# Evictions and rotations of the first attention block a step behind their pieces, the latent roots in four stages, another order of pieces

## The chip, the cores and the metric

The kernel runs on one core of a Trainium2 chip. The metric is the device time of one execution in microseconds, as the median of several runs. A core has TensorE (PE; matmuls, with a granted clock of 1.2 or 2.4 GHz), VectorE (DVE), ScalarE (ACT), GpSimd (POOL) and SyncE (SP, which issues the loads here). Each engine works through its own list of instructions in order; semaphores tie the lists together.

## The reference

Three transformer layers on 512 tokens of width 1024. The change lies in the mixer of the first:

```python
h = x @ w_in
c_q, c_kv, k_rope, q_s, k_s, v_s = _split(h, EVEN_SPLIT)      # 384, 256, 32, 512, 128, 128
q = (_rms_norm(c_q, q_norm) @ w_uq).reshape(B, S, 8, 64 + 32)
q_rope = _apply_rope(q[..., 64:], cos, sin)
kv = (_rms_norm(c_kv, kv_norm) @ w_ukv).reshape(B, S, 8, 64 + 64)
k_rope = _apply_rope(k_rope[:, :, None, :], cos, sin)[:, :, 0]
o_mla = _mla_attend(q_nope, q_rope, k_nope, k_rope, v)         # causal
o_swa = _swa_attend(q_s, k_s, v_s, sinks, rel_bias)            # window 128, 8 heads, 2 kv heads
m = jnp.concatenate([o_mla, o_swa], axis=-1) @ w_out
```

What follows (layer norms, MLPs, a second layer with forgetting attention, a third with four branches) is the same before and after.

## The kernel before

**Layout.** Activations stand transposed, features on the partitions and the 512 tokens in the free dimension. A weight tile is up to 8 blocks of 128 x 128. Each operand is split in a high and a low fp32r part: ScalarE writes the high part of a tile (WH, L357), VectorE the low part (WL, L363), and TensorE multiplies three times per block (L393 to L395: high by high, high by low of x, low by high). These three matmuls are a *piece*. A tile passes through one of four slots (RAW, WH, WL); `hi_ahead` and `lo_ahead` work three tiles ahead of the stream's tile `st.n`. Semaphores per slot are `loaded`, `hi_done`, `lo_done` and `used` (TensorE is through with the tile).

**Banks.** Linear outputs alternate between the PSUM banks 0 and 1 (`st.m % 2`). The first matmul of an output waits on `evac[b]` until the output before the last has been evicted. Evictions: VectorE for k, kr, uq and os; ScalarE for v, q, cq, ckv and ukv, the last in two copies, to K96 and VT. PB[2..3] hold scores, PB[4..5] transposed probabilities, PB[6] the values' result. PB[7] serves everything small, one user after the other in the order of `misc_keys` (`pe_misc` waits on `misc_free` of the one before): vector transposes, band turns, sums of squares ("var"), the products that swap halves for the rotation ("kswap", "qswap"), and turns of V ("v4").

**The attention loop.** 32 steps: sliding window (SWA) for 4 pairs of heads by 4 query blocks, then latent attention (MLA) the same. In step c, TensorE (`pe_attend`) does the scores of step c + 1, with query block 0 the values of the pair before, the transposes of step c (L494, which wait for the normalised probabilities, `probs_n`), and then `between(c)`: QUOTA[c] pieces from a list of work, FIRST before the loop, WITH_SWA in steps 0 to 15, WITH_MLA in 16 to 31. ScalarE copies transposed probabilities (L606) and makes exponentials (L582, L586), then runs `between(c)`. VectorE normalises step c (L597), takes the minimum or maximum of step c + 1 (L562, L568), subtracts the low half of an output at query block 0 (L626), then runs `between(c)`.

**Events.** ENDED[c] lists the pieces of work that end in step c. In `between(c)`, ScalarE and VectorE go through ENDED[c] in order; for each they first split the tile three ahead, then wait for TensorE to finish the piece, and evict it:

```python
            def mixer_between(c):
                for ev in ENDED[c]:
                    event(*ev)
```

"var" on VectorE is the reciprocal root (`rsqrt_dve`, L690 to L697) and the scalings of the latent (L2228); "split" the high and low parts of the scaled latent. `vectors` on VectorE copies the transposed vectors and prepares SINK, which the first SWA minimum reads.

SyncE loads the tiles in the order of TILES_A, which follows the lists, each when the low part of the tile four before is done; between the first four tiles and the rest it issues the band and 23 small loads.

## Time and profile before

| | us |
|---|---|
| median of 3 runs | 2456.65 (2456.44 to 2456.81) |
| profiled execution | 2457.71 |
| its span, first to last instruction | 2455.9 |
| TensorE busy | 2274.6 (93%) |
| mean granted clock of TensorE | 0.957 |
| first matmul of step 0's pieces | 56.33 |
| first output matmul from MLA's result (OMH) | 268.98 |

The profile is of one execution; times in it count from the first instruction. In the timeline each row is a start, a duration, the engine and line, and in brackets the idle time before it with what ended it. Matmuls overlap, so the distance of starts tells their rate.

### The profile page before, as it was taken

The page shows a single profiled execution, that of the slowest core. Times are in us where ns is not written, and L with a number is a line of the kernel's source. Part 1 is how long each engine was busy: PE and PEld are TensorE (multiplying, and loading weights), DVE is VectorE, ACT ScalarE, POOL GpSimd, SP SyncE. Part 2 cuts the span into 40 slices and gives each one's busy share as a digit, 9 for nine tenths or more (in the row PEclk, how much of TensorE's full clock was granted, in tenths as well). Part 3 has the DMA queues.
Part 4 walks back from the last instruction along what each step waited for, and adds up shares of the span by engine and source line. Part 5 has one row for each costly group of instructions (what it writes and reads, how often), then busy time and mean ns, then how long its engine had stood idle before and what let it go on. Part 6 is the DMA issues. An engine that isn't in the chain of part 4 may idle for free.

```text
span 2455.9 us, 28046 instructions
## 1 busy us (share of the span) xinstructions
PE 2274.6 (93%) x10190; PEld 1767.6 (72%) x10192; DVE 1263.6 (51%) x1966; ACT 895.2 (36%) x1479; POOL 368.3 (15%) x228
## 2 busy tenths in 40 slices
PE   7879799999999999899999888999969897999998
PEld 5646588888776676688888676467658675888886
DVE  4466553243464444642443664268569558443344
ACT  3444443143244453431332453322343233332333
POOL 0000420001320002400003500133022164000001
PEclk9999999999999999999999989879989898999999
DMA  5012133333233232233332332123211131333322
GB/s 163 17 36 65 52 86 103 102 94 96 67 93 107 69 86 69 69 102 103 92 97 81 91 90 71 35 62 98 74 39 56 43 99 52 104 88 107 95 70 77
DMA packets 360224, 196.43 MB, mean 80 GB/s; under 512 B 12575, under 2 KB 355372, under 8 KB 360124
## 3 DMA queue, kind: packets, MB, share of 16 engines
q1 hardware_dynamic: 360124, 195.10, 27.8%
q8 instruction: 62, 1.02, 0.2%
q14 instruction: 38, 0.31, 0.0%
HBM read 192.93 MB, written 2.14 MB: 79 GB/s over the span
## 4 chain that ended last, share of the span: by engine, by line
PE 81%; DVE 10%; ACT 4%; issue 2%; POOL 1%; SPq 1%; DMA 1%; DVEq 0%; ACTq 0%; POOLq 0%
PE PB L393 20%; PE PB L395 20%; PE PB L394 20%; PE PB L1284 3%; PE PB L1286 2%; PE PB L1285 2%; PE PB L494 2%; PE PB L475 2%; PE PB L521 1%; PE PB L1312 1%; PE PB L1361 1%; DVE WL L363 1%; ACT WH L357 1%; PE PB L1269 1%; ACT PR L582 1%
## 5 line engine op out<-in xcount | busy, mean ns | idle before, releaser
L393 PE MATMUL PB<-XH,WH 128*128 128x512 f32 (+1 forms) x1344 | 539.2, 401 | 45.1 <-DVE XL L785 23.2
L394 PE MATMUL PB<-XL,WH 128*128 128x512 f32 (+1 forms) x1344 | 532.0, 396 | 0.0
L395 PE MATMUL PB<-XH,WL 128*128 128x512 f32 (+1 forms) x1344 | 531.4, 395 | 0.0
L357 ACT ACTIVATE WH<-RAW 128x1024 fp32r<-128x1024 f32 (+2 forms) x379 | 380.3, 1007 | 411.3 <-PE PB L395 370.3
L373 DVE TENSOR_TENSOR WL<-RAW,WH 128x1024 fp32r<-128x1024 f32 x192 | 252.5, 1315 | 186.8 <-ACT WH L357 177.0
L393 PEld LDWEIGHTS PB<-XH,WH 128*128 128x128 f32 (+1 forms) x1344 | 257.3, 191 | 106.8 <-issue 48.7
L395 PEld LDWEIGHTS PB<-XH,WL 128*128 128x128 f32 (+1 forms) x1344 | 256.6, 191 | 56.7 <-issue 1.0
L394 PEld LDWEIGHTS PB<-XL,WH 128*128 128x128 f32 (+1 forms) x1344 | 257.3, 191 | 53.3 <-issue 0.8
L363 DVE TENSOR_TENSOR WL<-RAW,WH 128x1024 fp32r<-128x1024 f32 (+3 forms) x135 | 168.7, 1252 | 160.7 <-ACT WH L357 160.4
L395 PE MATMUL PB<-HH,WL 128*128 128x512 f32 x512 | 199.2, 389 | 0.0
L393 PE MATMUL PB<-HH,WH 128*128 128x512 f32 x512 | 199.2, 389 | 0.0
L394 PE MATMUL PB<-HL,WH 128*128 128x512 f32 x512 | 199.2, 389 | 0.0
L363 POOL TENSOR_TENSOR WL<-RAW,WH 128x1024 fp32r<-128x1024 f32 (+1 forms) x48 | 101.1, 2115 | 417.2 <-ACT WH L357 417.0
L751 POOL TENSOR_TENSOR SM<-ACC 128x512 f32<-128x512 f32 x4 | 5.2, 1292 | 917.7 <-DVE ACC L2287 532.5
L606 ACT ACTIVATE PT<-PB 128x256 f32<-128x256 f32 (+3 forms) x160 | 65.5, 411 | 166.0 <-PE PB L494 165.9
L1796 ACT ACTIVATE HS<-HR 128x512 f32<-128x512 f32 x64 | 40.5, 632 | 197.1 <-DVE HR L2305 197.1
L1284 PE MATMUL PB<-XH,WH 128*128 128x512 f32 x256 | 107.2, 419 | 4.6 <-ACT RS L1902 3.4
L394 PEld LDWEIGHTS PB<-HL,WH 128*128 128x128 f32 x512 | 96.1, 188 | 20.1
L395 PEld LDWEIGHTS PB<-HH,WL 128*128 128x128 f32 x512 | 96.1, 188 | 19.9
L393 PEld LDWEIGHTS PB<-HH,WH 128*128 128x128 f32 x512 | 96.1, 188 | 19.8
L494 PE MATMUL PB<-ID,PR 128*128 128x128 f32 x368 | 65.1, 295 | 41.8 <-DVE PR L597 41.1
L1285 PE MATMUL PB<-XL,WH 128*128 128x512 f32 x256 | 103.1, 403 | 0.0
(485 smaller groups left out, 3582.7 us busy)
## 6 DMA issues: line engine op xcount, KB each, us to landing
RAW<-in_w_up SPq DMA_DIRECT2D x64, 512.0 KB, 4.1
RAW<-in_w_down SPq DMA_DIRECT2D x64, 512.0 KB, 3.8
RAW<-in_w_ffn_gate_up SPq DMA_DIRECT2D x44, 512.0 KB, 3.8
RAW<-in_w_gate SPq DMA_DIRECT2D x32, 512.0 KB, 4.0
RAW<-in_od_w_in SPq DMA_DIRECT2D x24, 512.0 KB, 6.3
RAW<-in_w_in SPq DMA_DIRECT2D x24, 512.0 KB, 4.0
RAW<-in_ple_w_gate SPq DMA_DIRECT2D x16, 512.0 KB, 4.0
RAW<-in_w_ffn_down SPq DMA_DIRECT2D x16, 512.0 KB, 3.9
```

What stands on the lines that cost most here:

```text
L357: act.activation(WH[:, s, 0:nb], RAW[:, s, 0:nb], ACT.Copy).then_inc(hi_done[s], 1)
L363: eng.tensor_tensor(WL[:, s, 0:nb], RAW[:, s, 0:nb], WH[:, s, 0:nb].bitcast(F32), ALU.subtract).then_inc(lo_done[s], 1)
L373: dve.tensor_tensor(WL[:, s], RAW[:, s], WH[:, s].bitcast(F32), ALU.subtract).then_inc(lo_done[s], 1)
L393: pe.matmul(PB[b][0:m, 0:n], WH[:, s, k, 0:m], rh[:, kk, :], start=kk == 0, stop=False)
L394: pe.matmul(PB[b][0:m, 0:n], WH[:, s, k, 0:m], rl[:, kk, :], start=False, stop=False)
L395: x = pe.matmul(PB[b][0:m, 0:n], WL[:, s, k, 0:m], rh[:, kk, :], start=False, stop=kk == last)
L475: xs[e] = pe.matmul(PB[2 + e][:, lo:lo + w], q[:, qb * P:qb * P + P], k[:, ks[0] * P:ks[0] * P + w], start=True, stop=plain)
L494: x = pe.transpose(PB[4 + e][:, c * P:c * P + P], PR[:, e, c * P:c * P + P], ID[:])
L606: done(act.activation(PT[:, e, ks[0]:ks[0] + len(ks), qb * P:qb * P + P], PB[4 + e][:, 0:len(ks) * P].rearrange("p (j q) -> p j q", q=P), ...
L1284: pe.matmul(PB[m % 2][:], WH[:, n % 4, k], XH[:, k], start=k == 0, stop=False)
L1285: pe.matmul(PB[m % 2][:], WH[:, n % 4, k], XL[:, k], start=False, stop=False)
L1286: x = pe.matmul(PB[m % 2][:], WL[:, n % 4, k], XH[:, k], start=False, stop=k == DT - 1)
```

## The change

- The lists have another order: cq 0 is computed before the loop, ahead of the two vector transposes, which now come after the band turns; uq 2, 4 and 5 come earlier, turns and rotations are spread otherwise, and QUOTA is new (4, 4 and 2 pieces in steps 10 to 12, for example).
- In `between(c)`, ScalarE and VectorE first run the events of ENDED[c - 1], then split the tiles three ahead of those in ENDED[c] (`high_next`, `low_next`). An eviction, rotation or turn thus comes one step after its piece. Tile and bank are looked up by name (N_A, M_A).
- "var" and "split" become four stages: "var" (ScalarE's Ln and Exp), then one step later each "norm" (VectorE's root and scalings), "high" and "low". In ENDED they stand ahead of the pieces that end in the same step.

```diff
--- before.py
+++ after.py
@@ -785,29 +785,34 @@
...
-        FIRST = [("k", 0), ("v", 0), ("q", 0), ("q", 1)]
-        WITH_SWA = [("cq", 0), ("cq", 1), ("cq", 2), ("q", 2), ("ckv", 0), ("var", "cq"), ("ckv", 1), ("split", "cq"), ("q", 3),
-                    ("var", "ckv"), ("kr", 0), ("split", "ckv"), ("uq", 0), ("uq", 1), ("kswap", 0), ("qswap", 0), ("ukv", 0),
-                    ("qswap", 1), ("ukv", 1), ("uq", 2), ("uq", 3), ("qswap", 2), ("qswap", 3)]
-        WITH_MLA = [("v4", 0), ("ukv", 2), ("ukv", 3), ("os", 0), ("v4", 1), ("os", 1)]
-        WITH_MLA += [("uq", 4), ("uq", 5), ("qswap", 4), ("ukv", 4), ("qswap", 5), ("ukv", 5), ("os", 2), ("v4", 2), ("os", 3)]
-        WITH_MLA += [("uq", 6), ("uq", 7), ("qswap", 6), ("ukv", 6), ("qswap", 7), ("ukv", 7), ("os", 4), ("v4", 3)]
-        WITH_MLA += [("os", 5), ("os", 6), ("os", 7)]
-        PIECES = {"cq": 8, "ckv": 8, "q": 8, "kr": 8, "uq": 3, "ukv": 2, "os": 4, "split": 0}
-        QUOTA = [6, 6, 6, 6, 6, 6, 5, 6, 6, 5, 6, 6, 5, 4, 4, 4, 5, 5, 5, 5, 5, 4, 4, 4, 4, 4, 4, 3, 3, 3, 3, 3]
-        ENDED = [[] for _ in QUOTA]
-        c = total = 0
+        FIRST = [("k", 0), ("v", 0), ("q", 0), ("q", 1), ("cq", 0)]
+        WITH_SWA = [("cq", 1), ("cq", 2), ("q", 2), ("var", "cq"), ("ckv", 0), ("ckv", 1), ("q", 3), ("var", "ckv"), ("kr", 0),
+                    ("uq", 0), ("uq", 1), ("uq", 2), ("kswap", 0), ("qswap", 0), ("ukv", 0), ("qswap", 1), ("ukv", 1),
+                    ("uq", 3), ("qswap", 2), ("uq", 4), ("qswap", 3), ("uq", 5)]
+        WITH_MLA = [("v4", 0), ("ukv", 2), ("ukv", 3), ("qswap", 4), ("os", 0), ("os", 1), ("v4", 1), ("ukv", 4), ("qswap", 5), ("ukv", 5)]
+        WITH_MLA += [("uq", 6), ("uq", 7), ("v4", 2), ("os", 2), ("os", 3), ("qswap", 6), ("ukv", 6), ("qswap", 7), ("ukv", 7)]
+        WITH_MLA += [("os", 4), ("v4", 3), ("os", 5), ("os", 6), ("os", 7)]
+        PIECES = {"cq": 8, "ckv": 8, "q": 8, "kr": 8, "uq": 3, "ukv": 2, "os": 4}
+        QUOTA = [6, 6, 6, 6, 6, 6, 6, 6, 6, 6, 4, 4, 2, 4, 6, 5, 5, 5, 5, 3, 5, 4, 4, 5, 3, 2, 4, 3, 3, 3, 2, 2]
+        ENDED = [[] for _ in range(len(QUOTA) + 4)]
...
                 total += PIECES.get(ev[0], 1)
-                ENDED[next(c for c in range(len(QUOTA)) if sum(QUOTA[:c + 1]) >= total)].append(ev)
+                c = next(c for c in range(len(QUOTA)) if sum(QUOTA[:c + 1]) >= total)
+                ENDED[c].append(ev)
+                if ev[0] == "var":
+                    ENDED[c + 1].append(("norm", ev[1]))
+                    ENDED[c + 2].append(("high", ev[1]))
+                    ENDED[c + 3].append(("low", ev[1]))
...
         TILES_A = [ev for ev in IN_A if ev[0] != "os" or ev[1] % 2 == 0]
+        N_A = {ev: c for c, ev in enumerate(TILES_A)}
+        N_A.update({("os", o): N_A["os", o - 1] for o in range(1, DT, 2)})
         BLOCKS_A = {c: {"uq": 3, "ukv": 2}.get(ev[0], 8) for c, ev in enumerate(TILES_A)}
-        misc_keys = ["bandv", "vec", "vec2", "vs", *[("bandt", k) for k in range(4)]]
+        misc_keys = ["bandv", "vs", *[("bandt", k) for k in range(4)], "vec", "vec2"]
@@ -1480,18 +1485,19 @@
...
             lin1(8, XH, XL)
-            pe.wait_ge(sem["zeroed"], cnt.value("zeroed", "ones"))
-            pe.wait_ge(sem["small_in"], n_small)
-            pe.wait_ge(sem["x_cpa"], cnt.value("x_cpa", DT - 1))
-            pe_misc(pe, "vec", lambda: pe.transpose(PB[7][:, 0:P], VROW, ID[:]))
-            pe_misc(pe, "vec2", lambda: pe.transpose(PB[7][:, 0:P], VROW2, ID[:]))
...
             evac_of(pe, M_A["v", 0])
+            pe.wait_ge(sem["x_cpa"], cnt.value("x_cpa", DT - 1))
...
             pe.wait_ge(sem["band_in"], 16)
+            pe.wait_ge(sem["small_in"], n_small)
...
                 pe_misc(pe, ("bandt", k), lambda: pe.matmul(PB[7][:], CST[:, 0:P], BAND[:, 2 * k:2 * k + 2, :], start=True, stop=True))
+            lin1(8, XH, XL)
+            pe.wait_ge(sem["zeroed"], cnt.value("zeroed", "ones"))
+            pe_misc(pe, "vec", lambda: pe.transpose(PB[7][:, 0:P], VROW, ID[:]))
+            pe_misc(pe, "vec2", lambda: pe.transpose(PB[7][:, 0:P], VROW2, ID[:]))
@@ -1511,7 +1517,6 @@
...
                     x.then_inc(used[s], 1)
-                    st.n += 1
@@ -1519,6 +1524,7 @@
...
                 for what, i in events:
+                    st.n = N_A.get((what, i), st.n)
@@ -1557,8 +1563,7 @@
...
                         st.m += 1
-                    if what != "split":
-                        yield
+                    yield
@@ -1642,9 +1647,12 @@
...
+            n_last = len(TILES_A)
             for o in range(DT):
+                st.n = n_last + o // 2
...
                     pass
+            st.n += 1
@@ -1716,60 +1724,59 @@
...
-            def out_of_bank(*parts):
-                b, ub = st.bank(0)
+            def high_next(ev):
+                if ev in N_A and (ev[0] != "os" or ev[1] % 2 == 0):
+                    at_tile = Stream()
+                    at_tile.n = N_A[ev]
+                    hi_ahead(act, at_tile)
+            def out_of_bank(ev, *parts):
+                evac_n, b = N_A[ev], M_A[ev] % 2
+                act.wait_ge(used[evac_n % 4], evac_n // 4 + 1)
+                if ev[0] in ("cq", "ckv"):
+                    j = ev[1] if ev[0] == "cq" else 3 + ev[1]
+                    done(act.activation(SQC[:, j] if j < 3 else SQK[:, j - 3], PB[b][:], ACT.Square), "sq", j)
...
                 x.then_inc(evac[b], 1)
-                nxt()
...
-                if what in ("k", "uq"):
-                    skip()
-                elif what == "kr":
-                    skip()
-                elif what == "v":
-                    step()
-                    out_of_bank((VT[:], slice(0, P), 1.0))
+                if what == "v":
+                    out_of_bank((what, i), (VT[:], slice(0, P), 1.0))
                 elif what == "q":
-                    step()
-                    out_of_bank((QS[:, i], slice(0, P), -0.125))
+                    out_of_bank((what, i), (QS[:, i], slice(0, P), -0.125))
                 elif what in ("cq", "ckv"):
-                    step()
-                    b, ub = st.bank(0)
-                    j = i if what == "cq" else 3 + i
-                    done(act.activation(SQC[:, j] if j < 3 else SQK[:, j - 3], PB[b][:], ACT.Square), "sq", j)
-                    out_of_bank((ACC[:, j], slice(0, P), 1.0))
+                    out_of_bank((what, i), (ACC[:, i if what == "cq" else 3 + i], slice(0, P), 1.0))
                 elif what == "ukv":
-                    step()
-                    b, ub = st.bank(0)
...
                         act.wait_ge(sem["misc"], cnt.value("misc", ("v4", i // 2 - 1)))
-                    out_of_bank((K96[0:64, i], slice(0, 64), 1.0), (VT[i % 2 * 64:i % 2 * 64 + 64, :], slice(64, 128), 1.0))
+                    out_of_bank((what, i), (K96[0:64, i], slice(0, 64), 1.0), (VT[i % 2 * 64:i % 2 * 64 + 64, :], slice(64, 128), 1.0))
...
                     rsqrt_act(act, i, 384 if i == "cq" else 256, EPS5, bufs=LATB)
-                elif what == "split":
+                elif what == "high":
...
                         done(act.activation(CQH[:, j] if j < 3 else CKH[:, j - 3], ACC[:, j], ACT.Copy), "n_hi", j)
-                elif what == "os":
-                    if i % 2 == 0:
-                        hi_ahead(act, st)
-                    else:
-                        st.n += 1
-                    st.m += 1
             for ev in FIRST:
+                high_next(ev)
...
             def mixer_between(c):
+                for ev in ENDED[c - 1] if c else []:
+                    event(*ev)
                 for ev in ENDED[c]:
-                    event(*ev)
+                    high_next(ev)
             act_attend(act, ("swa", "mla"), 4, mixer_between)
+            for ev in ENDED[len(QUOTA) - 1]:
+                event(*ev)
+            st.n, st.m = len(TILES_A), M_IN + len(IN_A)
@@ -2193,26 +2200,28 @@
...
+            def low_next(ev):
+                if ev in N_A and (ev[0] != "os" or ev[1] % 2 == 0):
+                    at_tile = Stream()
+                    at_tile.n = N_A[ev]
+                    lo_ahead(dve, at_tile)
...
-                b, ub = st.bank(0)
-                if what in ("v", "q", "cq", "ckv", "ukv"):
-                    skip()
-                elif what == "k":
-                    step()
+                if (what, i) in N_A:
+                    n, b = N_A[what, i], M_A[what, i] % 2
+                if what in ("k", "kr", "uq"):
+                    dve.wait_ge(used[n % 4], n // 4 + 1)
+                if what == "k":
...
                     x.then_inc(evac[b], 1)
-                    nxt()
                 elif what == "kr":
-                    step()
                     dve.tensor_copy(KR[64:96, :], PB[b][0:32]).then_inc(evac[b], 1)
-                    nxt()
                 elif what == "uq":
-                    step()
                     dve.tensor_scalar(Q96[:, i], PB[b][0:96], -(96 ** -0.5), None, ALU.mult).then_inc(evac[b], 1)
-                    nxt()
@@ -2221,40 +2230,44 @@
...
                     token_major(("v4", i), V4[:, :, i * P:i * P + P])
-                elif what == "var":
+                elif what == "norm":
...
                         done(dve.scalar_tensor_tensor(ACC[:, j], ACC[:, j], VEC[:, g + j:g + j + 1], LATB[0][:], ALU.mult, ALU.mult), "norm", ("c", j))
-                elif what == "split":
+                elif what == "low":
...
                     if i % 2 == 0:
-                        lo_ahead(dve, st)
...
                     else:
-                        lin_ready(dve, st)
-                        st.n += 1
+                        dve.wait_ge(used[n % 4], n // 4 + 1)
                     dve.scalar_tensor_tensor(X[:, i], X[:, i], ALPHA, PB[b][:], ALU.mult, ALU.add).then_inc(evac[b], 1)
-                    st.m += 1
+            low_next(("k", 0))
             event("k", 0)
-            event("v", 0)
-            vectors()
-            event("q", 0)
+            low_next(("v", 0))
+            low_next(("q", 0))
             token_major("vs", VS[:])
-            event("q", 1)
+            low_next(("q", 1))
...
                 done(dve.tensor_scalar(BIAS[:, 2 * k:2 * k + 2, :], PB[7][:].rearrange("p (j n) -> p j n", n=256), -1.0, None, ALU.mult), "misc_free", ("bandt", k))
+            low_next(("cq", 0))
+            vectors()
             def mixer_between(c):
+                for ev in ENDED[c - 1] if c else []:
+                    event(*ev)
                 for ev in ENDED[c]:
-                    event(*ev)
+                    low_next(ev)
             dve_attend(dve, ("swa", "mla"), 4, mixer_between)
+            for ev in ENDED[len(QUOTA) - 1]:
+                event(*ev)
+            st.n, st.m = len(TILES_A), M_IN + len(IN_A)
```

## Rows read from the trace of the kernel before

**Rows 1.** The profile's page: busy time, and the chain that ended last.

```profile
PE 2274.6 (93%) x10190; PEld 1767.6 (72%) x10192; DVE 1263.6 (51%) x1966; ACT 895.2 (36%) x1479; POOL 368.3 (15%) x228
...
PE 81%; DVE 10%; ACT 4%; issue 2%; POOL 1%; SPq 1%; DMA 1%; DVEq 0%; ACTq 0%; POOLq 0%
```

**Rows 2.** Windows: us, busy PE, PEld, DVE, ACT, POOL, PEclk, DMA, GB/s.

```profile
53.60:95.00 41.40, 40.23 (x211) 29.40 (x210) 20.24 (x71) 21.94 (x61) 0.00 (x0) 1.00 0.07 16
95.00:111.00 16.00, 10.09 (x62) 7.58 (x62) 8.13 (x25) 2.93 (x9) 0.00 (x0) 0.79 0.01 4
```

**Rows 3.** Waits of PE, 44 to 272 us: total, times, longest.

```profile
PE PB L494 <- DVE PR L597: 24.4, 12, 5.9
PE PB L1552 <- DVE ROT L2186: 4.2, 2, 2.4
```

**Rows 4.** Timeline of PE and ACT, 28 to 54 us: start, duration, [idle before].

```profile
28.36 0.40 PE L395 MATMUL PB<-XH,WL 128*128 128x512 f32 x1
28.59 0.28 PE L1486 MATMUL PB<-ID,VROWS 128*128 128x128 f32 x1
...
30.59 1.06 ACT L357 ACTIVATE WH<-RAW 128x1024 fp32r<-128x1024 f32 x1 [7.81 <-DMA RAW<-in_ev_w_in]
...
33.28 0.48 PE L1487 MATMUL PB<-ID,VROWS 128*128 128x128 f32 x1 [4.41 <-DVE VEC L2164]
...
35.26 0.63 PE L394 MATMUL PB<-XL,WH 128*128 128x512 f32 x1
35.69 0.63 PE L395 MATMUL PB<-XH,WL 128*128 128x512 f32 x1
...
53.60 0.49 PE L475 MATMUL PB<-K,QS 64*128 64x128 f32 x4
```

**Rows 5.** Timeline of PE, 56 to 269 us.

```profile
56.33 0.47 PE L393 MATMUL PB<-XH,WH 128*128 128x512 f32 x1
...
61.68 0.47 PE L393 MATMUL PB<-XH,WH 128*128 128x512 f32 x1
...
101.56 1.15 PE L494 MATMUL PB<-ID,PR 128*128 128x128 f32 x4 [5.91 <-DVE PR L597]
...
128.04 1.15 PE L494 MATMUL PB<-ID,PR 128*128 128x128 f32 x4 [4.98 <-DVE PR L597]
...
147.19 1.07 PE L1552 MATMUL PB<-Q,CST 96*96 96x512 f32 x2 [1.81 <-DVE ROT L2186]
...
151.96 0.44 PE L494 MATMUL PB<-ID,PR 128*128 128x128 f32 x2 [2.39 <-DVE PR L597]
...
261.85 1.25 PE L494 MATMUL PB<-ID,PR 128*128 128x128 f32 x8 [3.29 <-DVE PR L597]
...
268.98 0.50 PE L1507 MATMUL PB<-OMH,WH 128*128 128x512 f32 x1
```

**Rows 6.** Timeline of DVE at the first latent root.

```profile
96.05 0.69 DVE L690 TENSOR_SCALAR LATB<-PB 128x512 f32<-128x512 f32 x1 [2.45 <-ACT LATB L682]
...
98.97 2.08 DVE L2228 SCALAR_TENSOR_TENSOR ACC<-ACC,VEC,LATB 128x512 f32<-128x512 f32 x3
```

**Rows 7.** Groups of DVE by form, 44 to 272 us: busy us, mean ns.

```profile
L2214 DVE TENSOR_SCALAR Q<-PB 96x512 f32<-96x512 f32 x8 | 5.4, 680 | 0.0
...
L626 DVE TENSOR_TENSOR OSL<-PB,OSH 128x512 fp32r<-128x512 f32 x4 | 2.8, 689 | 3.2 <-ACT OSH L619 3.2
...
L2186 DVE TENSOR_TENSOR TMP<-PB,CST 32x512 f32<-32x512 f32 x4 | 2.8, 689 | 0.6 <-issue 0.5
```

**Rows 8.** Groups of ACT by form, 44 to 272 us.

```profile
L1722 ACT ACTIVATE VT<-PB 64x512 f32<-64x512 f32 x8 | 4.8, 594 | 0.1
L1722 ACT ACTIVATE K<-PB 64x512 f32<-64x512 f32 x8 | 4.7, 588 | 1.8 <-PE PB L395 1.7
```

**Rows 9.** Timeline of ACT, one MLA step.

```profile
178.16 0.39 ACT L606 ACTIVATE PT<-PB 128x256 f32<-128x256 f32 x1 [0.36 <-PE PB L494]
...
180.04 0.42 ACT L357 ACTIVATE WH<-RAW 128x256 fp32r<-128x256 f32 x1
```

## Prediction, made before the changed kernel ran

> **What bounds the kernel now.** I read the page first: TensorE is busy 93% of the span, and the chain that ended last runs through it for 81% [rows 1]. The reader is to see that a microsecond in which TensorE stands still, or runs at the lower clock, is a microsecond of the end. Next the windows of the first attention block: from 53.6 to 95 TensorE is busy 40.23 of 41.40 us at granted clock 1.00, from 95 to 111 only 10.09 of 16.00 at 0.79 [rows 2]. So the loss is lumpy, and the waits say where. From 44 to 272 us TensorE waits 24.4 us in front of its transposes (L494) for VectorE's normalised probabilities (L597), and 4.2 us for rotations (L1552) [rows 3]: 28.6 us. TensorE's timeline gives the single stalls: 4.41 us before the second vector transpose (33.28), then 5.91 and 4.98 behind the two latent roots, 1.81 and 2.39 around the first rotations, 3.29 in the last step, with smaller ones between [rows 4, 5]; the twelve for L597 sum to the 24.4.
>
> The price of the lower clock is in the same timeline: starts are 0.23 us apart at 2.4 GHz (28.36 to 28.59) and 0.43 at 1.2 GHz (35.26 to 35.69) [rows 4]. Behind the stall of 4.41 ten matmuls start so, 2.0 us lost. Inside the attention I found five such stretches, behind the stalls of 5.91, 4.98, 1.81 with 2.39, 2.16 and 3.29: about 2.0 us each, 10.1 in all. Stalls of 1.2 to 2.4 us that stood alone had none.
>
> **The change, part by part.**
>
> *The start.* Before, the second vector transpose waits for VectorE's copy of the first, which is queued behind the low part of tile 4, and that behind a load. The pair moves behind the band turns and the eight pieces of ("cq", 0). The stall (4.41), its slow matmuls (2.0) and the pair itself (0.4) leave; the cq tile joins at 24 starts of 0.2275 = 5.46, the pair again with one copy between at 0.8. The scores of step 0 then start at 53.60 - 6.8 + 6.3 = 53.1 instead of 53.60. VectorE now has VEC2, SINK and HB directly in front of its first minimum; that takes back 0.1, so the first piece comes at 55.9 instead of 56.33 [rows 4, 5], with 5.46 us of work already done. Gain 5.9. Loads don't change this: ScalarE could split tile 4 at 30.59, and it is needed only at 46.6; SyncE issues the tiles in the new order of the list, each behind the low part four tiles back, as before, and its small loads keep their place. TensorE's wait for them moves from after the second tile to the band turns, long after they landed.
>
> *Method for the rest.* I replayed the 32 steps, from one step's first piece to the next: quota x 0.685 plus scores and transposes (56.33 to 61.68 is 6 pieces and 1.23 us) [rows 5], and carried the VectorE and ScalarE queues along in their new order. Work of TensorE is the same but for cq 0. What changes are the waits. Four groups:
>
> (a) Latent roots. VectorE's part is still one block: 2.92 us of root (96.05 to 98.97) and 2.08 for three scalings [rows 6]. It no longer waits for Ln and Exp, and low parts come later. cq: in step 6, with 4.1 us of pieces against it, a stall of 1.85 remains in front of step 7. ckv: in step 10 the list of VectorE is [norm ckv, kr, ...]: the eviction of kr stands behind the root. TensorE needs kr's bank for ("uq", 1) after one piece (0.7); VectorE is at the minimum until 0.5, root to 3.4, two scalings to 4.8, kr 0.68 to 5.5. Stall 4.85, and 0.85 in step 11 for uq 0's bank. Sum 7.55, in place of 5.91 + 1.19 + 4.98 = 12.1.
>
> (b) Rotations and turns, one step behind, all through PB[7]. In step 12 the quota is 2 and its first piece, qswap 0, waits for the first product of kswap's rotation: after the values TensorE needs 0.5, VectorE the output half (ScalarE 0.6, then 0.69), two low parts 1.3, uq 2 0.68, the product 0.69 [rows 7]: 3.9. Stall 3.45. The same count gives 0.5 (step 13), 0.5 (15), 2.25 + 0.25 (16, v4 behind qswap 3), 1.2 (17), 0.3 (19), 0.9 (24): 9.35, in place of 7.4 (1.81, 2.39, 2.36 and three small ones). GpSimd's copies of the rotated key still start after kswap and are done before the MLA scores.
>
> (c) ukv evictions. Now ScalarE evicts a ukv piece a step later, behind two copies and two exponentials (178.16 to 180.04, 1.9 us) [rows 9], in 0.588 + 0.594 us [rows 8]. With two banks the piece after next needs that bank, and ukv has two pieces. Step 14: from the transposes on 1.9 for ScalarE's block, 0.2 because the maximum comes late, 1.18 for ukv 0: uq 3 waits 3.25; os 0 in step 17 waits 0.7, uq 6 in step 20 1.4, uq 7 in step 21 2.9: 8.25. None of this is in the trace of before, where TensorE waited for no bank of ScalarE. From below it is nothing (if ScalarE's queue has slack that I don't see), from above four times the whole block less the scores' cover, 1.9 + 2 x 1.18 = 4.3: 17.2. I take 8.25, since the queue is strict and its durations stand in rows. The Trainium skill, "Perfetto Trace Analysis", section Matmuls, says that independent matmul groups should rotate through banks so that the eviction of one overlaps the matmuls of the next. Before keeps to it with two banks; the change moves away from it. By it alone (c) would sit at its upper bound, and the time at 2460.
>
> (d) The end of MLA, where VectorE's low part waits for ScalarE's high part, which waits behind exponentials: 1.05 (step 23), 0.65 (25), 2.45 (26: between two transposes TensorE has two pieces, 1.4, and 1.8 of scores; ScalarE has 1.9, ukv 7 with 1.2 and a high part of 1.05, then VectorE 1.2 of low part and 0.5 of normalising), 0.4 + 1.9 (27), 0.6 (30), 0.9 (31): 7.95, in place of 1.21 + 1.45 + 0.96 + 2.16 + 3.29 = 9.1.
>
> Stalls: 7.55 + 9.35 + 8.25 + 7.95 = 33.1 against 28.6, +4.5. Clock: I expect five slow stretches again, behind 4.85, 3.45, 3.25, 1.4 with 2.9, and 2.45 with 1.9: 10.0, of which 3.8 fall on waits that end at a fixed time anyway (0.85, 0.5, 0.5, 1.9), so 6.2 against 10.1, -3.9. Together with the start: -5.9 + 4.5 - 3.9 = -5.3. The output matmuls would start at 263.7 instead of 268.98 [rows 5]; behind that nothing changes. The profiled execution took 2457.71 (span 2455.9), 1.1 above the median of the runs, 2456.65; the difference goes onto the median: 2451.4.
>
> **Rivals.** 0.2% is 4.9 us, about what a measurement of this kernel can tell from no change; the bounds are 2451.7 and 2461.6.
>
> 1. As computed, 2451.4, own range 2447.5 to 2455: chance 0.45. For it: start and latent roots are read from rows. Against: (b) to (d) are small differences of long queues.
> 2. Nothing gained: the new bank and PB[7] waits give the start's gain back. If (b) comes at 1.5 times my count (+4.7), 2456.1. Chance 0.17, range 2453 to 2461.
> 3. Better: the evictions behind a step hide in slack of ScalarE. Without (c) and the one stretch of low clock that only it brings, -10.3: 2441.1; half of it 2446. Chance 0.25. Against it speaks that quotas of 2 and 3 leave TensorE little to do while the queues catch up.
> 4. Slower: each ukv pair costs its upper bound, 17.2 instead of 8.25, and one more stretch at 1.2 GHz at each of two places where I expect none (os 0, uq 6), 4.0: +12.9, 2464. It decides from +10.2, that is when TensorE waits over 14 us for ScalarE's evictions. Chance 0.13. The skill's rule on banks, in the page named above, points this way.
>
> The range 2440 to 2461.5 leaves out 0.07 of case 3 and case 4 with 0.13. Under 2451.7 lie some 0.28 of case 1 and 0.23 of case 3: 0.51 faster. Over 2461.6 lies case 4, 0.13: slower. The same: 0.36.
>
> **What would show it.** No stall of TensorE between 28 and 40 us, and no starts 0.43 apart there; the vector pair after cq 0, under 0.8 us. One stall of about 2 us for VectorE's probabilities where 5.91 stood; one of 4 to 5 us in front of ("uq", 1)'s first matmul, released by kr's eviction (the line of KR<-PB). A stall of 3 us or so at qswap 0; stalls at the first matmul of uq 3 and uq 7, released by ScalarE's line that writes VT. The total of TensorE's waits for probabilities well below 24.4, since they move to bank and PB[7] waits. The output matmuls from OMH start between 260 and 267. The prediction is wrong if TensorE passes uq 3 and uq 7 without a stall (then case 3), or if stalls that I have at 1 to 2 us prove 3 and pull the clock down (case 4), or if the granted clock elsewhere in the program shifts by more than two stretches.

## The result, and the profile after

The kernel after takes 2461.05 us (median of 20 runs, 2457.79 to 2466.67), beside 2456.98 of the kernel before in the same comparison (20 runs): 1.0016 times its time, 95% interval [1.0009, 1.0022]. That is 4.1 us more, 0.16%, where 5.3 less had been forecast. It lies in the range given, near its upper end, but the sign is wrong.

The page of after, busy time and chain, beside [rows 1]:

```profile
PE 2278.1 (93%) x10192; PEld 1768.6 (72%) x10192; DVE 1262.9 (51%) x1966; ACT 894.6 (36%) x1479; POOL 367.3 (15%) x228
...
PE 82%; DVE 9%; ACT 5%; issue 2%; POOL 1%; DMA 0%; SPq 0%; DVEq 0%; ACTq 0%; POOLq 0%
```

TensorE still sets the end, and its busy time has grown by 3.5 us with hardly a matmul more. Over the whole program the lower clock explains only 0.5 of it: half of TensorE's busy time in the stretches at 1.2 GHz is 74.7 us against 74.2, that is 3.2 more in the attention, 2.5 less at the start and 0.2 less behind. (The ledger below comes to the rest.) The windows of after (us, busy PE, PEld, DVE, ACT, POOL, PEclk, DMA, GB/s) say where:

```profile
28.00:53.60 25.60, 22.86 (x94) 16.40 (x92) 9.11 (x11) 6.20 (x9) 0.00 (x0) 1.00 0.60 150
53.60:95.00 41.40, 38.87 (x202) 27.71 (x203) 19.49 (x75) 20.29 (x59) 0.00 (x0) 1.00 0.06 15
95.00:111.00 16.00, 14.39 (x86) 9.98 (x84) 10.62 (x30) 8.08 (x24) 0.00 (x0) 1.00 0.03 8
111.00:136.00 25.00, 19.63 (x98) 11.07 (x98) 14.48 (x48) 9.02 (x27) 0.00 (x0) 0.86 0.11 29
136.00:158.00 22.00, 15.72 (x58) 8.96 (x55) 14.77 (x36) 8.73 (x26) 4.62 (x8) 0.77 0.12 37
158.00:176.00 18.00, 14.76 (x85) 10.94 (x84) 11.73 (x26) 5.17 (x17) 0.00 (x0) 0.91 0.15 46
176.00:195.00 19.00, 16.91 (x75) 11.75 (x74) 10.60 (x25) 9.06 (x24) 0.00 (x0) 0.91 0.05 15
195.00:220.00 25.00, 19.50 (x96) 12.89 (x94) 14.12 (x33) 10.67 (x27) 0.00 (x0) 0.93 0.27 85
```

And the same view of before, from 136 on, which [rows 2] did not reach:

```profile
136.00:158.00 22.00, 17.63 (x91) 10.43 (x89) 16.65 (x42) 9.30 (x29) 5.53 (x8) 0.92 0.14 43
158.00:176.00 18.00, 14.84 (x91) 10.19 (x89) 13.16 (x34) 8.65 (x26) 0.00 (x0) 1.00 0.09 24
176.00:195.00 19.00, 18.85 (x94) 13.19 (x94) 12.04 (x32) 9.33 (x25) 0.00 (x0) 1.00 0.19 54
195.00:220.00 25.00, 22.30 (x114) 15.14 (x112) 15.92 (x39) 11.12 (x32) 0.00 (x0) 1.00 0.21 67
```

The window from 95 to 111, the worst of before at 10.09 busy and 0.79 [rows 2], is now 14.39 at 1.00, and the start is free of its stall. From 136 to 220 the change gives it back: TensorE is busy for 66.89 us instead of 73.62, at a granted clock of 0.77, 0.91, 0.91, 0.93 in place of 0.92 and three times 1.00.

The waits of PE from 44 to 272 us in after (total, times, longest), beside [rows 3]:

```profile
PE PB L494 <- DVE PR L597: 10.0, 11, 1.9
PE PB L393 <- ACT VT L1742: 6.7, 3, 2.8
PE PB L393 <- DVE KR L2222: 4.6, 1, 4.6
PE PB L1558 <- DVE ROT L2193: 4.4, 2, 3.7
PE PB L1147 <- DVE ROT L2193: 2.5, 1, 2.5
...
PE PB L1558 <- DVE V L2201: 1.3, 1, 1.3
```

The waits for the probabilities fell from 24.4 to 10.0 us. In their place stand waits for evictions and turns that come a step late: VT from ScalarE, and KR, ROT and V from VectorE. TensorE's timeline gives the places that answer to [rows 4, 5]:

```profile
53.80 0.49 PE L475 MATMUL PB<-K,QS 64*128 64x128 f32 x4
...
56.54 0.47 PE L393 MATMUL PB<-XH,WH 128*128 128x512 f32 x1
...
100.12 0.90 PE L494 MATMUL PB<-ID,PR 128*128 128x128 f32 x4 [1.59 <-DVE PR L597]
...
125.14 0.74 PE L393 MATMUL PB<-CQH,WH 128*96 128x512 f32 x1 [4.56 <-DVE KR L2222]
...
131.11 0.47 PE L393 MATMUL PB<-CQH,WH 128*96 128x512 f32 x1 [0.79 <-DVE Q L2224]
...
140.64 1.14 PE L1558 MATMUL PB<-Q,CST 96*96 96x512 f32 x1 [3.66 <-DVE ROT L2193]
...
153.32 0.74 PE L393 MATMUL PB<-CQH,WH 128*96 128x512 f32 x1 [2.62 <-ACT VT L1742]
153.85 0.63 PE L394 MATMUL PB<-CQL,WH 128*96 128x512 f32 x1
154.28 0.63 PE L395 MATMUL PB<-CQH,WL 128*96 128x512 f32 x1
...
271.98 0.50 PE L1513 MATMUL PB<-OMH,WH 128*128 128x512 f32 x1
```

The output matmuls start at 271.98 instead of 268.98. The row at 125.14 is uq 1 and that at 131.11 uq 2, the stall of 3.66 us is where qswap 0 was said to wait, 153.32 is uq 3, and the matmuls behind that one (153.85, 154.28) start 0.43 us apart, the spacing of 1.2 GHz.

The ledger up to those output matmuls. **Idle** is the sum of TensorE's gaps from the first scores on; **clock loss** is half of TensorE's busy time in the stretches whose granted clock is the lower level. Both are summed from the instructions and the clock records of the traces.

| us | before | after | forecast of the difference | measured |
|---|---|---|---|---|
| start: first piece of step 0, less 5.46 for cq 0 done | 56.33 | 56.54 (-5.46) | -5.9 | -5.25 |
| idle | 30.2 | 34.1 | +4.5 | +3.9 |
| clock loss in the attention | 10.0 (5 stretches) | 13.1 (7 stretches) | -3.9 | +3.15 |
| not assigned | | | | +1.2 |
| output matmuls of OMH | 268.98 | 271.98 | -5.3 | +3.0 |

Behind that point both lose the same to the clock (60.3 and 60.1 us). Start and idle came out within 0.7 us of the forecast. The clock missed by 7.

The 1.2 that is not assigned goes with the number of gaps. A matmul is shown for 0.39 us while the next in a row starts 0.23 behind it, so the one ahead of each gap adds some 0.16 of busy time. From the first piece to the output matmuls, less idle, clock loss and cq 0, the time is 168.2 us in before with 15 gaps over 0.1 us, 169.4 in after with 24; in the experiments below 168.6 with 15 (e12), 168.9 with 19 (e6) and 170.0 with 26 (e5). Nine gaps at 0.16 would be 1.4: this is an estimate, and no run changes the number of gaps alone.

### The profile page after: what moved, and what is told of

Read it like the earlier page. It is cut to its first block, busy times and chain, and to the rows that moved or that the text cites. A ratio compares the mean times of both kernels' runs of the same rounds, so it can differ in the third digit from the quotient of the medians.

```text
span 2458.7 us, 28047 instructions
## 1 busy us (share of the span) xinstructions
PE 2278.1 (93%) x10192; PEld 1768.6 (72%) x10192; DVE 1262.9 (51%) x1966; ACT 894.6 (36%) x1479; POOL 367.3 (15%) x228
## 4 chain that ended last, share of the span: by engine, by line
PE 82%; DVE 9%; ACT 5%; issue 2%; POOL 1%; DMA 0%; SPq 0%; DVEq 0%; ACTq 0%; POOLq 0%
PE PB L393 20%; PE PB L395 20%; PE PB L394 20%; PE PB L1289 3%; PE PB L1291 2%; PE PB L1290 2%; PE PB L475 2%; PE PB L521 2%; PE PB L494 2%; PE PB L1317 1%; PE PB L1366 1%; DVE WL L363 1%; ACT WH L357 1%; PE PB L1274 1%; ACT PR L582 1%
## 5 line engine op out<-in xcount | busy, mean ns | idle before, releaser
L1291 PE MATMUL PB<-XH,WL 128*128 128x512 f32 x256 | 103.1, 403 | 0.0
```

The costliest lines, as they stand in the source:

```text
L1291: x = pe.matmul(PB[m % 2][:], WL[:, n % 4, k], XH[:, k], start=False, stop=k == DT - 1)
```

## The experiments

Eleven kernels were changed and one was run again. Each was compared with before on the same chip; its medians there were 2457.11, 2456.48 and 2456.60. Idle, clock loss and the number of stretches are from each kernel's one profiled execution, up to the output matmuls, counted as in the ledger. (The recorded expectations call after's idle 34.5: that has 0.4 which the vector pair waits ahead of the first scores.)

| kernel | median us | ratio to before, 95% | idle | clock loss (stretches) | OMH at |
|---|---|---|---|---|---|
| before | 2456.98 | | 30.2 | 10.0 (5) | 268.98 |
| after | 2461.05 | 1.0016 [1.0009, 1.0022] | 34.1 | 13.1 (7) | 271.98 |
| e1 start only | 2453.75 | 0.9983 [0.9975, 0.9992] | 30.4 | 10.5 (5) | 265.13 |
| e2 all but the start | 2463.76 | 1.0031 [1.0019, 1.0043] | 34.2 | 11.0 (6) | 275.16 |
| e3 root last | 2459.18 | 1.0009 [0.9999, 1.0019] | 33.1 | 12.6 (6) | 271.21 |
| e4 ukv in its step | 2446.73 | 0.9952 [0.9939, 0.9964] | 25.7 | 6.9 (3) | 257.83 |
| e5 turns in their step | 2464.86 | 1.0029 [1.0021, 1.0038] | 35.7 | 14.0 (6) | 276.22 |
| e6 all in its step | 2445.72 | 0.9953 [0.9940, 0.9965] | 24.1 | 8.0 (4) | 257.02 |
| e8 ukv 0 to 3 in step | 2455.74 | 0.9995 [0.9985, 1.0004] | 31.4 | 6.2 (3) | 261.80 |
| e9 evictions in step, root last | 2443.79 | 0.9947 [0.9932, 0.9961] | 24.2 | 4.3 (2) | 253.43 |
| e10 waits filled | 2457.79 | 1.0005 [0.9996, 1.0014] | 26.6 | 6.5 (3) | 266.96 |
| e11 all in step, root last | 2445.30 | 0.9960 [0.9947, 0.9972] | 23.6 | 6.0 (3) | 254.08 |
| e12 old order, staged roots | 2445.21 | 0.9959 [0.9947, 0.9971] | 21.0 | 11.3 (5) | 256.33 |
| e13 after again | 2461.02 (1 run) | | 34.2 | 12.0 (6) | 270.93 |

### e1: the start alone, e2: all but the start

e1 is before with cq 0 and the vector pair at their new places, and quotas one lower in the first eight steps. e2 is after with before's start and eight quotas one higher.

```
e1:
-        FIRST = [("k", 0), ("v", 0), ("q", 0), ("q", 1)]
+        FIRST = [("k", 0), ("v", 0), ("q", 0), ("q", 1), ("cq", 0)]
-        QUOTA = [6, 6, 6, 6, 6, 6, 5, 6, 6, 5, ...
+        QUOTA = [5, 5, 5, 5, 5, 5, 4, 5, 6, 5, ...
e2 (against after):
-        QUOTA = [6, 6, 6, 6, 6, 6, 6, 6, 6, 6, ...
+        QUOTA = [7, 7, 7, 7, 7, 7, 7, 7, 6, 6, ...
```

> The kernel before with the start alone: cq 0 and the vector pair moved ahead of the loop, its eight pieces taken from the quotas of steps 0 to 7, events in the old scheme. Theory A (the start gives what the trace of the changed kernel shows, 5.25 us; the loss lies in the waits and the clock of the rest): 4 to 5.5 us under before, no stall between 28 and 40 us, waits in the loop 28 to 31 us and five stretches at 1.2 GHz as before. Theory B (the gain of the start is only lent, since thinner steps leave the latent roots uncovered): under 2 us, and the stalls at the roots longer by what is missing in pieces.

> The changed kernel with the old start (cq 0 in the loop, one piece more in steps 0 to 7). Theory A: the sum is plain, so 7 to 9 us over before and about 5 over the changed kernel; the waits at uq 1, qswap 0, uq 3, v4 and uq 7 unchanged within 0.3. Theory B: 3 to 5 over before.

e1 is 3.4 us faster than before; in its trace the first piece of step 0 starts at 56.67 with cq 0 done, a gain of 5.1, of which 3.85 is left at the output matmuls (265.13 against 268.98): idle rose from 30.16 to 30.45, the clock loss by 0.5. So the start's gain is kept to three quarters, not merely lent. e2 is 6.7 us slower than before. Both medians lie between the two theories, nearer A (4 to 5.5 under and 7 to 9 over before). The rest of the change is therefore the fault, and it costs more than the 0.6 that the forecast had for it (+4.5 of waits less 3.9 of clock).

### e4: only the ukv evictions back in their own step

```
 for ev in ENDED[c - 1] if c else []:
-    event(*ev)
+    if ev[0] not in ("ukv",):
+        event(*ev)
 for ev in ENDED[c]:
     high_next(ev)
+    if ev[0] in ("ukv",):
+        event(*ev)
```

> The changed kernel, but ScalarE evicts ukv pieces in their own step. Theory A (evictions behind a step cost bank waits and, through them, clock): the 6.7 us of waits for the line that writes VT go, with two stretches at 1.2 GHz (behind uq 3 and uq 7), about 3.3; ScalarE is later with copies and exponentials in four steps, which gives 1 to 2 back: 6 to 9 under the changed kernel. Theory C (the order of the pieces is at fault, a wait removed in one place stands in the next): under 2.

One edit turns the loss into a gain: 14.3 us less than after, where theory A gave 6 to 9. Both engines' lists are changed in this way, but ukv pieces are evicted by ScalarE alone. The waits of PE, 44 to 272 us, in e4:

```profile
PE PB L494 <- DVE PR L597: 9.2, 13, 1.6
PE PB L393 <- DVE KR L2226: 4.6, 1, 4.6
PE PB L1558 <- DVE ROT L2197: 4.5, 2, 3.7
PE PB L1147 <- DVE ROT L2197: 2.5, 1, 2.5
```

The row of VT is gone and no other has grown: idle fell by 8.4 us. The clock fell with it, from seven stretches to three, 6.2 us. The windows of e4 that hold uq 3, uq 6 and uq 7:

```profile
136.00:158.00 22.00, 18.02 (x92) 11.10 (x86) 16.69 (x43) 9.42 (x30) 4.62 (x8) 0.84 0.12 37
...
176.00:195.00 19.00, 18.71 (x97) 13.03 (x96) 11.63 (x29) 8.01 (x25) 0.00 (x0) 1.00 0.11 35
195.00:220.00 25.00, 22.30 (x113) 15.01 (x111) 16.11 (x38) 11.95 (x32) 0.00 (x0) 1.00 0.26 85
```

8.4 + 6.2 = 14.6, less 0.6 for a start that came later in this execution, is 14.0; the output matmuls start 14.1 earlier. Why the late eviction makes TensorE wait is in ScalarE's timeline of after:

```profile
151.59 0.50 ACT L582 ACTIVATE PR<-SW,STAT 128x257 f32<-128x257 f32 x1
...
152.08 0.58 ACT L1742 ACTIVATE K<-PB 64x512 f32<-64x512 f32 x1
152.67 0.59 ACT L1742 ACTIVATE VT<-PB 64x512 f32<-64x512 f32 x1
```

The bank that uq 3 needs is emptied at 152.67 to 153.26, behind the step's copies and exponentials, and uq 3 starts at 153.32.

### e8: ukv 0 to 3 in their step, ukv 4 to 7 late

```
against e4:
-    if ev[0] in ("ukv",):
+    if ev[0] == "ukv" and ev[1] < 4:
```

> The kernel after with ukv 0 to 3 evicted in their own step, and ukv 4 to 7 a step behind as after. Theory A (each stretch at 1.2 GHz belongs to the wait ahead of it): the 2.6 us wait in front of uq 3 and the 0.5 in front of os 0 go, and with them the stretches that stood at 153 and 180 us, while the waits of 1.2 and 2.8 us in front of uq 6 and uq 7 stay with the stretch at 208 us: 3 to 4 us of waits and 1.6 to 3.3 us of clock less, 2454 to 2457. Rival (the loss of clock is that of the average load and comes back elsewhere): only the waits are gained, still seven stretches, 2457 to 2459.

The median, 2455.7, is theory A's. The waits are as it said: those at uq 3 and os 0 are gone, 1.24 and 2.82 at uq 6 and uq 7 remain; idle fell by 2.7, the median by 5.3. But the profiled execution was the fastest of the twelve (2448.7), and it has no stretch behind the 2.82 at uq 7 nor behind the 2.46 at v4, where after has one, while it has one at 100.4 behind the 1.61 of the first root, where after has none behind 1.59. The waits were the same and the clock was not. So a stretch doesn't belong to its wait strictly, and of the median only the size speaks for A here.

### e3: the second root behind kr's eviction

```
+        for done_here in ENDED:
+            done_here.sort(key=lambda ev: ev[0] == "norm")
```

> The kernel after with one change: where a latent root ends in the same step as pieces, the pieces' evictions come first on both engines, so VectorE evicts kr before it computes the second root. Theory A (each wait of TensorE costs its own length, and a wait of this size is followed by a stretch at 1.2 GHz): the 4.6 us wait in front of uq 1 and the 0.8 behind it go, and a wait of 2 to 4 us appears in front of the next chunk's transposes, because the probabilities now come behind the root; sum of waits 1 to 3 us less, stretches as many as before: 2458 to 2460. Theory C (the order of the pieces is at fault, not who evicts when): no change, 2460 to 2462.

As A said: the wait for KR falls from 4.56 to 0.39, one of 2.68 for the probabilities comes in front of the next transposes, idle falls by 1.0 and the median by 1.9, from 2461.05 to 2459.18. On its own chip e3 is 2.7 us over before, after was 4.1 over: this difference is too small for these runs to tell.

### e5, e6 and e11: turns and everything in their own step

The edit is that of e4, with ("kswap", "qswap", "v4") in e5 and every kind of piece in e6; e11 is e6 with e3's sorting.

> The kernel after with the turns of kswap, qswap and v4 taken off PB[7] in their own step, the evictions still a step behind. Theory A says that VectorE is the engine that is short here, so that the 9.3 us of waits for ROT, V and TMP go and come back as waits for the probabilities (PR) of about the same length, as in the kernel with everything in its own step, where 9 us of the one were replaced by 11 us of the other: waits within 2 us of after's 34.5, time 2458 to 2463. Rival: the late turns are as dear as the late evictions on ScalarE, and 5 us or more of waits go, with one or two stretches: below 2455.

> The changed kernel with every eviction, rotation and turn in its own step; the four stages of the roots, the order and the start stay. Theory A: waits in the loop 22 to 27 us instead of 34.5 and four or five stretches at 1.2 GHz instead of seven: 10 to 15 under the changed kernel, 6 to 11 under before. Theory C (the new order of pieces and quotas costs it, not the delay): waits in the loop stay over 31 and the time within 3 of the changed kernel.

> The kernel after with every eviction, rotation and turn in its own step and the latent root behind the pieces of its step. Against e9 (turns of PB[7] a step behind, 2443.8) it tells what the late turns are worth where nothing else is late. Theory A (VectorE is short there, the wait only changes its name): waits of 24 to 26 us in the loop as there, 2443 to 2446. Rival: the late turns were of use, because VectorE reaches the probabilities first: 2447 or more, with waits of 28 us or more.

e5 is 3.8 us slower than after. Waits of PE, 44 to 272 us, in e5:

```profile
PE PB L494 <- DVE PR L597: 16.5, 16, 2.8
...
PE PB L393 <- DVE Q L2228: 2.0, 2, 1.2
PE PB L1513 <- issue: 2.0, 1, 2.0
PE PB L393 <- DVE CKL L2246: 2.0, 1, 2.0
```

and in e6:

```profile
PE PB L494 <- DVE PR L597: 20.8, 18, 3.7
PE PB L393 <- DVE CKL L2246: 2.0, 1, 2.0
```

In e5 the 9.3 us for ROT, V and TMP went, and the wait for PR grew from 10.0 to 16.5, with 2.0 for CKL, 2.0 at os 0 (L1513) instead of 0.5 and 2.0 for Q instead of 0.8: VectorE does the same work, and what stands ahead in its queue only decides which of its products TensorE waits for. The idle rose by 1.6, within A's 2 us, but the median lies above A's 2463. e6 is 1.0 us from e4 although it moves all of VectorE's work as well; it is 15.3 under after, where A gave 10 to 15. As far as these runs can tell, of the late evictions, rotations and turns only one group costs, ScalarE's. e11 against e9 (below) says the same: 23.6 against 24.2 of idle, 2445.3 against 2443.8.

### e9: evictions in their step, turns late, root last

```
against e4:
-    if ev[0] in ("ukv",):
+    if ev[0] in ("ukv", "kr", "uq"):
```

with e3's sorting.

> The kernel after with all evictions of ukv, uq and kr in their own step, and the latent root behind them in its step; the turns of PB[7] stay a step behind. Theory A: against the kernel with ukv alone in its own step (2446.7), the waits for KR and Q, 5.4 us, go, and 2 to 4 us come back in front of the transposes behind the root: 2443 to 2446. Rival (VectorE is short, so that the work only changes its place): 2446 to 2449.

2443.79, as theory A had it, and the fastest kernel: 0.9947 times before [0.9932, 0.9961], 12.7 us on the same chip. Waits of PE, 44 to 272 us:

```profile
PE PB L494 <- DVE PR L597: 14.2, 14, 3.7
PE PB L1560 <- DVE ROT L2199: 3.9, 3, 3.1
```

KR and Q are gone, one wait of 3.7 stands behind the second root.

### e12: the old order of pieces

```
 WITH_SWA, WITH_MLA: the lists of before, less ("cq", 0) and the splits
-    ENDED[c + 1].append(("norm", ev[1]))      (high at c + 2, low at c + 3)
+    ENDED[c].append(("norm", ev[1]))          (high at c + 1, low at c + 2)
 QUOTA: that of e1
```

with everything in its own step and e3's sorting, as in e11.

> The start of after, the order of pieces and the quotas of before (less cq 0, which is in the start), everything in its own step, the roots in stages a step apart. It differs from e11 in the order of the pieces and in the root's stages lying one step earlier. Theory A (order is worth little; the staged root gives back the 5.2 and 5.0 us waits of e1 less 1.6 and 3.7): waits about 26 us, clock loss 5 to 8, 2444 to 2448. Theory C (the other order is itself the gain or the fault): more than 3 us away from e11 in one direction or the other.

2445.21 beside 2445.30 of e11. The other order is worth nothing that these runs can tell, so theory C falls, unless the stages that lie one step earlier here hide what the order costs; that was not separated. A had the median, but not by its terms (26 us of idle and 5 to 8 of clock; 21.0 and 11.3 came). Against e1 it gains 8.5 us, mostly at the roots, now in stages and behind their step's pieces: their 5.21 and 4.97 us waits are 1.55 and 2.39 here. Its profiled execution has the least idle of all and still 11.3 us of clock loss, more than kernels with 3 to 10 us more idle: idle alone doesn't fix the loss of one execution.

### e10: the same waits, filled with work

TensorE gets matmuls whose result nobody reads, in front of three pieces that wait; nothing else differs from after.

```
+ if i in (1, 6, 7):
+     last = ("var", "ckv") if i == 1 else ("qswap", 5)
+     pe.wait_ge(sem["misc_free"], cnt.value("misc_free", last))
+     for _ in range({1: 18, 6: 5, 7: 12}[i]):
+         pe.matmul(PB[7][:], CQH[:, 0, 0:P], CQH[:, 0, :], start=True, stop=True)
  yield from lin_parts(pe, st, [3], CQH, CQL, 96)
```

> The kernel after, with the same order, the same steps of every eviction and the same waits, but TensorE is given work whose result nobody reads while it waits: 18 matmuls of 512 columns into PB[7] ahead of uq 1 (4.6 us of wait in after, 18 x 0.21 = 3.8 us of work), 5 ahead of uq 6 (1.2 us of wait) and 12 ahead of uq 7 (2.8 us). They take no wait away: the pieces still start when KR and VT have been evicted. Theory A (the loss of clock comes from TensorE standing still): idle time falls by 6 to 7 us to about 27, and with it two or three of the seven stretches at 1.2 GHz go: 3 to 6 us faster than after, 2455 to 2458. Rival D (the stretches come with the load or at places of their own, whatever TensorE did before): the time of after within 1.5 us, 2459.5 to 2462.5, seven stretches.

The timeline of PE in e10:

```profile
121.01 4.39 PE L1539 MATMUL PB<-CQH 128*128 128x512 f32 x18 [0.28 <-DVE LATB L690]
125.30 0.48 PE L393 MATMUL PB<-CQH,WH 128*96 128x512 f32 x1
125.61 0.40 PE L394 MATMUL PB<-CQL,WH 128*96 128x512 f32 x1
...
129.43 0.47 PE L393 MATMUL PB<-CQH,WH 128*96 128x512 f32 x1 [0.79 <-DVE Q L2229]
```

and its windows:

```profile
111.00:136.00 25.00, 23.21 (x127) 13.96 (x125) 15.03 (x49) 10.05 (x30) 0.00 (x0) 1.00 0.11 29
136.00:158.00 22.00, 16.09 (x48) 9.03 (x49) 14.96 (x36) 7.76 (x24) 5.08 (x8) 0.77 0.12 36
...
176.00:195.00 19.00, 16.89 (x85) 11.32 (x84) 11.84 (x29) 9.07 (x24) 0.00 (x0) 1.00 0.11 30
195.00:220.00 25.00, 23.11 (x118) 16.72 (x115) 14.81 (x34) 12.47 (x33) 0.00 (x0) 1.00 0.28 90
```

uq 1 starts at 125.30 as before the filling (125.14), but from 111 to 136 the granted clock is 1.00 instead of 0.86, and from 195 to 220 1.00 instead of 0.93. What that is worth stands in the timeline: uq 2, with the same wait of 0.79, starts 4.13 us behind uq 1 here and 5.97 in after. No piece was released earlier (uq 7 starts 3.43 us behind its step's transposes in both), and the two stretches that went behind uq 1 and uq 7 had cost 2.1 and 1.6 us. Of the windows left alone, 136 to 158 and 158 to 176 stay at 0.77 and 0.91, but 176 to 195 is at 1.00 too instead of 0.91, with the same waits of 1.30 and 0.50 in it, and so is the window from 243 on, as in e13. So of the 6.6 us less of clock loss (6.5 instead of 13.1, three stretches instead of seven) 3.7 stood where a wait was filled; the others may have gone by the filling or by the difference between executions.

Rival D gave at least 2459.5 and seven stretches; it falls by both, but the medians alone would leave it open: e10 is 3.3 us below after and, each against the before of its own comparison, 2.9, with intervals that touch ([0.9996, 1.0014] and [1.0009, 1.0022]). The output matmuls start 5.0 us earlier. That is less than 6.6; 0.4 of it is that the filling runs past the wait at uq 6 (one of these matmuls took 0.24 us, not 0.21). The median gains less still, and more is lost to the clock behind the attention (62.5 us against 60.1, though e13 has 62.5 too).

### e13: after once more

> The kernel after once more, for a second profiled execution of the same program. If the stretches at 1.2 GHz belong to the waits ahead of them, the single waits are the same to 0.1 us and there are again six to eight stretches; if the loss of clock differs from execution to execution with the same waits, the count differs by more than that, and the spread of after's own times (2457.8 to 2466.7) is this term.

The single waits repeat to 0.02 us (4.56, 3.66, 2.62, 2.46, 2.82), and idle to 0.1. The stretch that after had at 248.8 is missing. The window of e13:

```profile
243.00:269.00 26.00, 22.27 (x117) 15.03 (x117) 13.95 (x35) 12.76 (x33) 0.00 (x0) 1.00 0.18 49
```

After's first execution has 0.93 in this one. Six stretches and seven, 12.0 and 13.1 us, from one program with the same waits. The Trainium skill, "TensorE: Matmul & The Clock Gate", Part 1, says that the number of matmuls at the lower clock when a kernel starts differs from run to run of the same kernel. In these two executions the number of stretches differs inside the kernel too.

## Why the prediction was wrong, by its own steps

**The step that failed is the clock term**: "I expect five slow stretches again ... 10.0, of which 3.8 fall on waits that end at a fixed time anyway, so 6.2 against 10.1, -3.9". Measured: 13.1 us in seven stretches (12.0 in six). The five that it named were all there, behind uq 1, qswap 0, uq 3, uq 7 and the step of 1.65 and 1.95 us. Two came that it did not have, at 170.2 beside v4's 2.46 us, and at 180.5 behind 1.30 and 0.50. It had taken from before that stalls of 1.2 to 2.4 us cost no clock. And of the 3.8 that were to fall on four waits little did. The wait of 0.79 at uq 2 (forecast 0.85) is as long in e10 without a stretch, so the 1.8 us between the two kernels there are lost in full; it is shorter, 0.33 and 0.44, only in e2 and e8, where more is lost behind uq 1 (2.9 and 2.8 us instead of 2.1). The wait of 0.79 at 161.9 (0.5) is 0.80 in e4 with no stretch ahead of it, and that of 1.95 in step 27 (1.9) came ahead of its stretch, not behind. Only step 13's (0.5) was hidden: it is 0.62 in e2, e3 and e8, which lose 1.7 us behind qswap 0, and gone in after, e13 and e4, which lose 2.9 or 3.0 (in e10 too, with 1.7 lost a little further on). Two stretches more, about 3.1, and the 3.8 booked as hidden make the 7; the 0.6 that did hide is in the idle row.

**The waits** were right. (a) 1.59, 4.56 and 0.79 against 1.85, 4.85 and 0.85; kr's eviction stands directly behind the root, as VectorE's timeline of after shows:

```profile
122.96 1.42 DVE L2237 SCALAR_TENSOR_TENSOR ACC<-ACC,VEC,LATB 128x512 f32<-128x512 f32 x2
124.41 0.68 DVE L2222 COPY KR<-PB 32x512 f32<-32x512 f32 x1
```

(b) 3.66 at qswap 0, 2.46 at v4 and 1.30 at step 17, against 3.45, 2.25 and 1.2. (c) 2.62 at uq 3, 0.50 at os 0, 1.24 and 2.82 at uq 6 and uq 7, 7.2 against 8.25; e4 showed that what hangs on it is worth 8.4 of idle. The bank rule of the Trainium skill ("Perfetto Trace Analysis", Matmuls) named the right place. The upper bound that the prediction tied to it, 17.2, is not what these waits cost, but with its clock the breach cost 14.3 us, e4 against after. (d) 1.65 and 1.95 at the end instead of 2.45 and 1.9, the wait of 3.29 [rows 5] gone. Two waits were not foreseen, 0.60 and 0.71 in front of the transposes at 72.7 and 93.1.

**The start** brought 5.25 at the first piece instead of 5.9: the scores begin at 53.80, not 53.1. The stall and its slow matmuls are gone as computed (no wait over 0.8 us from 28 to 54 us, granted clock 1.00), and the pair waits 0.38 once. The missing 0.65 is smaller than what executions differ by: in the kernels with this same start the first scores begin between 52.64 (e8) and 55.24 (e5).

**The rivals.** Case 3, that (c) hides in slack, is excluded: its waits were there. What case 3 priced for their absence, 10.3, was 14.3 in e4. Case 4 had its mechanism wrong (7.2, not 17.2 us of waits for ScalarE) and the number of its side effect right, two stretches more than expected, but only one of them at a place that it named: at os 0 (180.5), the other at v4 and not at uq 6. Case 2 had the outcome, the start's gain given back, by the wrong term: (b) cost what was computed.

**What an idle microsecond costs.** Against after, the medians moved by 14.3 for 8.4 us of idle (e4), 5.3 for 2.7 (e8), 1.9 for 1.0 (e3), 15.3 for 10.0 (e6), 17.3 for 9.9 (e9) and 15.8 for 10.5 (e11); e5 +3.8 for +1.6. That is 1.5 to 2.3 us of time for one of idle, where the sum had taken 1; the four large differences alone give 1.5 to 1.8. e12, with the other order, lies below: 15.8 for 13.1, 1.2. With 1.7 for the +4.5 and no separate clock term, the forecast would have been -5.9 + 7.7 = +1.8, no change that can be told; the 1.7 is read from the same runs, so this is no test of it.

**Open:** the 1.2 us of the ledger, for which the gaps are an estimate only, and which wait brings a stretch in which execution (e8 has none at uq 7, e12 has five for 21 us of idle). Taking the stretch at v4 or at qswap 0 away alone was not tried. That idle time ahead costs clock is shown by e10 at uq 1 and uq 7, 3.7 of after's 13.1 us; for the other stretches it is argued from their places behind waits. The factor is read from medians of seven kernels of one loop, on more than one chip.

## What to carry to other kernels

Work that empties a bank for TensorE must not stand behind a whole step of its engine's other work if the banks are only two: check, for each eviction moved, which piece needs that bank next and how much TensorE has to do until then. When TensorE is as busy as here (93%), don't forecast the clock by counting the large stalls: in this loop each new microsecond of idle cost one and a half to two, and slow stretches booked as hidden were mostly not. A moved eviction on the engine that is short (VectorE here) mostly renames the wait, while one on an engine with slack makes a new one; so undo it per engine before judging a change as a whole.

## What was unexpected of the hardware

Unused matmuls in a wait that can't be removed gave time back: 35 matmuls of 512 columns in three waits, 5.0 us at the output matmuls and about 3 in the median. The lower clock also came behind stalls that were short: at 180.5 us after 1.30 and 0.50 us in after and e13 (not in e10, with the same two), and at 248.8 after 1.65 and 1.95, there in one execution of two.
